# Mixer of a hybrid block: attention pairs two slots behind, bias and maximum in one VectorE instruction, scaling and gate on GpSimd, norms on ScalarE

## The chip, the cores and the metric

The kernel runs on one NeuronCore of one Trainium2 chip. The metric is the device time of one execution in microseconds; lower is better. Six phases run one after the other: pool0, conv, mla, pool1, mixer, ffn. The change touches the mixer alone, and, at its edges, the way the phase in front of the ffn is entered.

## The reference, cut to what matters

The mixer takes 512 tokens of 1024 features, projects them to 27 tiles of 128 columns, and computes three things from them: sliding-window attention with sinks (4 heads of 64), block attention with a linear distance bias (4 heads of 64), and a gated delta rule (4 heads of 128) in chunks of 64 tokens.

```python
scores = jnp.einsum('bnqhgd,bnshd->bnhgqs', qb, kk) * (d ** -0.5)
scores = scores - m * rel                                  # linear bias, masked outside the window
mx = jnp.maximum(scores.max(axis=-1, keepdims=True), sink)
p = jnp.exp(scores - mx)
denom = p.sum(axis=-1, keepdims=True) + jnp.exp(sink - mx)
...
qkv_c = jax.nn.silu(causal_depthwise_conv_2(qkv_c, dn_conv_w))
qc = l2_norm(qc);  kc = l2_norm(kc)                        # x * rsqrt(sum(x*x) + eps), per head
...
def step(state, xs):                                       # one chunk of 64 tokens
    v_new = u_c - w_c @ state
    o = qd_c @ state + a_c @ v_new
    state = state * exp(gl_c) + kd_c.T @ v_new
...
o_c = rms_norm_2(o_c, dn_norm) * jax.nn.silu(z_c)
mixed = jnp.concatenate([o_a, o_b, o_c], axis=-1);  return mixed @ w_out
```

With 512 tokens every block of 256 keys that lies before a query is selected, so the block attention is plain causal attention with the bias.

## The kernel before, in words

Everything lies in SBUF as features x tokens, in tiles of 128 x 512. A projection tile is a product of 8 blocks; each block is three fp32r matmuls (L626 to L628: high part by high, high by low, low by high). The weights stream through a ring of four slots: a DMA on SyncE fills `w_stage`, ScalarE copies it to `w_hi` (L1152, `his(n)`), GpSimd subtracts to `w_lo` (L569, `lo_units`), TensorE uses both and frees the slot. ScalarE works its queue in order, so where `his` stands among its other work decides when the next weights are there; it runs up to four units ahead, and a tile takes two.

The order of the mixer's work is written out by hand in `mixer_steps()`, which lists the steps of TensorE, VectorE and ScalarE; each step raises a semaphore of its engine and the others wait for its number.

- **Front** (`project_in(13)` L668, VectorE L1813 to L1817, ScalarE L1330 to L1339): 8 tiles that pass a causal convolution of width 4 on VectorE (`conv_tile`, L1799: one take, one tensor_scalar, three L1807), a SiLU and a square on ScalarE; one tile for beta and decay; 4 more convolution tiles. The first three tiles are made together, block by block.
- **Delta products** (`delta_products`, L895): the other 14 tiles with the sums of squares (`ssk`, `ssq`), the transpose of the beta and decay rows (`rowt`, L909), and the products of the delta rule in between. ScalarE takes the square roots of the norms (L1359, L1363), VectorE the reciprocals (L1834) and multiplies (L1836, L1838).
- **Inverse** (`inverse`, L941): five levels of 128 x 128 products (L888) for the triangular inverse of all heads.
- **Chunk loop** (L1070): per chunk c the state recurrence `nv` (L978, L981) -> `vn` (ScalarE, L1440) -> `o` and `su` (L989, L993, L999) -> `st` (VectorE, L1971), and two attention pairs k = 2c and 2c + 1 of 16. A pair is two heads of one block of 128 queries, over w = 128 to 512 keys. `attend` (L1004) makes the scores (L1019) and adds the bias as a second matmul of a scaled identity with a distance table (L1021). VectorE reduces the maximum (L1956) and corrects it (L1959 to L1963), ScalarE takes the exponentials with their sums (L1416), VectorE divides (L1948, L1950), TensorE transposes (L1033), ScalarE copies (L1427), TensorE multiplies with the values (`values`, L1050), ScalarE copies to `mixed` (L1435). The scores of pair k, the transpose of k - 1 and the values of k - 2 share a slot.
- **Tail** (L1085 to L1096): two more rounds for the last pairs, the norm of the delta output (`osqrt`, `orc`, `ornt` L1091, `orn`, `ob` L1095), its gain and gate on VectorE (L2001, L2003), the split of `mixed` into parts (`act_h` L1461, `act_l` L1990), and the out projection, tile after tile.

In SWA pairs (k < 8) both heads of a pair lie in the same half of the partitions and their scores in one PSUM bank; in the pairs from 8 on they lie in different halves and banks.

Of the kernel before, what the change touches and what calls it, by code (L numbers as in the profile page):

```python
# [147 lines left out]

HEADS = range(4)
CHUNKS = S // CHUNK  # L150
PAIRS = 16


def mixer_steps():
# [6 lines left out]
    dve = ["ydt", ("kf", 0), ("kf", 1), "beta", "g", ("kf", 2), ("kf", 3), "cols", ("qf", 0), "cd"] + each("kb")  # L161
    dve += [("qf", 1)] + each("dt") + [("qf", 2), ("qf", 3)] + each("kbe") + each("lt", "xt0") + each("at")
    dve += each("e1") + each("qd")
    act = ["tanh", "e1", "ln", "nega"] + each("sk") + each("sq") + each("zs") + ["cexp", "ckd"] + each("egl", "edt")
    act += each("vb") + each("kd") + each("xc") + each("eg")
    for l in range(1, LEVELS):
        pe += each(f"y{l}") + each(f"p{l}")
        dve += (each(f"e{l + 1}") if l < LEVELS - 1 else []) + each(f"xt{l}")
        act += each(f"yc{l}")
    pe += each("wt")  # L170
    act += each("nw")
    dve += ["slopes"]
# [4 lines left out]
    def attend(k):  # L177
        if 1 <= k <= PAIRS:
            dve.append(("nr", k - 1))
        if k < PAIRS:  # L180
            pe.append(("s", k))
            dve.append(("mx", k))
            act.append(("ex", k))

    def turn(k):
        if 1 <= k <= PAIRS:
            pe.append(("t", k - 1))
            act.append(("pc", k - 1))

    def values(k):  # L190
        if 2 <= k:
            pe.append(("pv", k - 2))
            act.append(("mc", k - 2))

    for c in range(CHUNKS):
        act += [("vn", c)]
        attend(2 * c)
        pe += [("nv", c)]
        turn(2 * c)
        pe += [("o", c)] + ([("su", c)] if c < CHUNKS - 1 else [])  # L200
        act += [("oc", c)]
        dve += [("st", c)] if c < CHUNKS - 1 else []
        if c % 2:
            act += [("osq", c // 2)]
        values(2 * c)
        attend(2 * c + 1)
        turn(2 * c + 1)
        if c % 2:
            pe += [("osum", c // 2)]
        values(2 * c + 1)  # L210
    for k in (PAIRS, PAIRS + 1):
        attend(k)
        turn(k)
        values(k)
    pe += ["ornt"] + each("ob")
    act += ["osqrt"]
    dve += ["orc", "orn"] + each("on")
# [34 lines left out]
def program(nc, x_in, stream, params_in, consts_in, consts2_in, pos_in, out, phases):  # L252
    ctx = ExitStack()
    with ctx:
# [26 lines left out]
        probs = sb("probs", [P, 2, 2, S], F32, late)  # L281
        slope_ident = sb("slope_ident", [P, 8, P], F32, late)
# [13 lines left out]
        w_lo = sb("w_lo", [P, RING, S], F32R)  # L296
# [308 lines left out]
        def _(pe):  # L605
# [431 lines left out]
            def values(k):  # L1037

                if k < 2:
                    return  # L1040
# [1242 lines left out]
```

## Time and profile before

| | us |
|---|---|
| runs shown | 2353.81, 2356.09, 2356.20 (median 2356.09) |
| profiled execution, its own time | 2356.29 |
| its span, first to last instruction | 2354.5 |
| TensorE busy | 2269.4 (96%) |
| VectorE / ScalarE / GpSimd busy | 1206.3 / 886.3 / 1031.4 |
| mean granted TensorE clock | 0.981 of full |

The mixer lies from about 1503 to about 1947 us of the span. The granted clock has two levels: 1.00 is 2.4 GHz, 0.50 is 1.2 GHz, and a stretch between is a mean of both.

### The profile page before, as it was taken

To read this page: it belongs to the slowest core of one execution; us is meant where nothing else is said; L and a number is where in the kernel's file an instruction comes from. 1 tells how busy PE (TensorE), PEld (TensorE's weight loads), DVE (VectorE), ACT (ScalarE), POOL (GpSimd) and SP (SyncE) were. 2 spreads that over 40 slices of the span, in tenths; PEclk is the share of its full clock that TensorE was granted. 3 is DMA by queue.
4 is the path that set the end of the run, shared out by engine and by line. 5 is a ranking of instruction groups with operands and counts; after the bars stand their busy time and mean duration, and the time that the engine had idled before them with its cause. 6 is when DMAs were issued, how large, how long until landed. Compare 5 with 4: busy or idle time off the path is not lost.

```text
span 2354.5 us, 32284 instructions
## 1 busy us (share of the span) xinstructions
PE 2269.4 (96%) x10448; PEld 1816.3 (77%) x10448; DVE 1206.3 (51%) x1573; ACT 886.3 (38%) x1546; POOL 1031.4 (44%) x753
## 2 busy tenths in 40 slices
PE   8999999999999999999999999989999887999996
PEld 6788888888888887777887888776896565777785
DVE  7832234444432635555267223496754348888613
ACT  4343343344343434444333443334423323323322
POOL 5654444544544444443456544443200032555553
PEclk9999999999999999999999999999999889999998
DMA  3332323233222222111322322222100021222332
GB/s 133 98 99 98 98 91 99 96 98 98 98 96 96 95 93 72 54 63 36 99 90 89 107 98 93 101 89 72 55 1 1 1 72 45 90 97 89 102 104 98
DMA packets 53643, 194.46 MB, mean 83 GB/s; under 512 B 6080, under 2 KB 6336, under 8 KB 53568
## 3 DMA queue, kind: packets, MB, share of 16 engines
q1 hardware_dynamic: 52560, 191.13, 24.8%
q10 hardware_dynamic: 1008, 2.33, 0.3%
q8 instruction: 47, 0.77, 0.1%
q14 instruction: 28, 0.23, 0.0%
HBM read 191.34 MB, written 2.10 MB: 82 GB/s over the span
## 4 chain that ended last, share of the span: by engine, by line
PE 49%; issue 35%; POOL 15%; DVE 1%; POOLq 1%; ACT 0%; ACTq 0%; DVEq 0%
POOL w_lo L569 15%; PE proj L626 13%; PE proj L627 13%; PE proj L628 13%; PE aux L771 1%; PE proj L796 1%; PE proj L725 1%; PE proj L727 1%; PE proj L726 1%; PE aux L774 1%; PE aux L782 1%; PE proj L753 0%; PE proj L755 0%; PE proj L754 0%; PE proj L743 0%
## 5 line engine op out<-in xcount | busy, mean ns | idle before, releaser
L569 POOL TENSOR_TENSOR w_lo<-w_stage,w_hi 128x512 fp32r<-128x512 f32 x716 | 990.4, 1392 | 1226.1 <-ACT w_hi L1152 1225.5
L1152 ACT ACTIVATE w_hi<-w_stage 128x512 fp32r<-128x512 f32 x716 | 437.1, 627 | 761.9 <-PE proj L628 706.3
L626 PE MATMUL proj<-xh,w_hi 128*128 128x512 f32 x1696 | 672.6, 397 | 19.0 <-POOL w_lo L569 16.9
L627 PE MATMUL proj<-xl,w_hi 128*128 128x512 f32 x1696 | 662.0, 390 | 0.0
L628 PE MATMUL proj<-xh,w_lo 128*128 128x512 f32 x1696 | 661.8, 390 | 0.0
L626 PEld LDWEIGHTS proj<-xh,w_hi 128*128 128x128 f32 x1696 | 319.3, 188 | 106.0 <-POOL w_lo L569 34.1
L628 PEld LDWEIGHTS proj<-xh,w_lo 128*128 128x128 f32 x1696 | 319.1, 188 | 67.6
L627 PEld LDWEIGHTS proj<-xl,w_hi 128*128 128x128 f32 x1696 | 319.5, 188 | 66.8 <-issue 2.4
L626 PE MATMUL proj<-act_h,w_hi 128*128 128x512 f32 (+1 forms) x864 | 337.7, 391 | 0.6 <-POOL w_lo L569 0.6
L627 PE MATMUL proj<-act_l,w_hi 128*128 128x512 f32 (+1 forms) x864 | 336.9, 390 | 0.0
L628 PE MATMUL proj<-act_h,w_lo 128*128 128x512 f32 (+1 forms) x864 | 336.9, 390 | 0.0
L626 PEld LDWEIGHTS proj<-act_h,w_hi 128*128 128x128 f32 x864 | 162.7, 188 | 37.5 <-issue 2.5
L628 PEld LDWEIGHTS proj<-act_h,w_lo 128*128 128x128 f32 x864 | 162.7, 188 | 33.9
L627 PEld LDWEIGHTS proj<-act_l,w_hi 128*128 128x128 f32 x864 | 162.8, 188 | 33.5
L1220 ACT ACTIVATE act_h<-prod 128x512 f32 (+1 forms) x102 | 64.5, 632 | 258.9 <-DVE prod L2037 130.9
L1566 DVE TENSOR_TENSOR ssum<-ssum,sq 128x512 f32<-128x512 f32 x64 | 63.9, 998 | 150.5 <-ACT sq L1158 150.1
L1607 DVE TENSOR_TENSOR x_res<-proj,x_res 128x512 f32 x32 | 22.1, 692 | 218.3 <-PE proj L628 217.1
L1637 DVE TENSOR_TENSOR act_l<-prod,act_h 128x512 f32 (+1 forms) x102 | 82.0, 804 | 85.8 <-ACT act_h L1220 85.8
L2043 DVE TENSOR_TENSOR z<-proj,rstd 128x512 f32<-128x512 f32 x32 | 22.1, 692 | 112.7 <-PE proj L628 111.9
L583 POOL TENSOR_SCALAR pr<-pr,small 128x128 f32<-128x128 f32 (+3 forms) x32 | 40.8, 1275 | 76.0 <-DVE small L1737 76.0
L1267 ACT ACTIVATE pr<-aux,small 128x128 f32<-128x128 f32 (+3 forms) x64 | 33.2, 524 | 53.2 <-DVE small L1730 53.1
L2086 DVE SCALAR_TENSOR_TENSOR yg<-gpad,params_sb,yg 128x512 f32<-128x512 f32 x44 | 49.9, 1133 | 6.5 <-DVE yg L2084 3.4
(313 smaller groups left out, 2413.4 us busy)
## 6 DMA issues: line engine op xcount, KB each, us to landing
w_stage<-stream SPq DMA_DIRECT2D x358, 512.0 KB, 3.3
out<-x_res SPq DMA_DIRECT2D x4, 512.0 KB, 2.6
x_res<-x SPq DMA_DIRECT2D x2, 512.0 KB, 8.3
consts_sb<-consts ACTq DMA_DIRECT2D x1, 832.0 KB, 4.4
x_res<-x ACTq DMA_DIRECT2D x1, 512.0 KB, 7.4
x_res<-x SPq DMA_DIRECT2D x1, 256.0 KB, 3.3
x_res<-x ACTq DMA_DIRECT2D x1, 256.0 KB, 5.1
pos_i<-pos ACTq DMA_DIRECT2D x1, 256.0 KB, 2.7
```

The costliest lines, as they stand in the source:

```text
L569: pool.tensor_tensor(w_lo[:, at, :], w_stage[:, at, :], w_hi[:, at, :].bitcast(F32), ALU.subtract).then_inc(stage_free, 1)
L583: pool.tensor_scalar(pr[:, qb % 2, 0, 0:w], pr[:, qb % 2, 0, 0:w], stat(INVERSE, qb)[:, 0:1], None, ALU.mult).then_inc(probs_done, 1)
L626: pe.matmul(o, w_hi[:, slot, cols], hi, start=(b == 0), stop=False)
L627: pe.matmul(o, w_hi[:, slot, cols], lo, start=False, stop=False)
L628: mm = pe.matmul(o, w_lo[:, slot, cols], hi, start=False, stop=(b == blocks - 1))
L725: pe.matmul(o, w_hi[:, slot, cols], lat_h[:, k, :], start=(b == 0), stop=False)
L1152: act.activation(w_hi[:, u % RING, :], w_stage[:, u % RING, :], ACT.Copy).then_inc(hi_done, 1)
L1220: act.activation(act_h[:, slot, :], prod[:, :], ACT.Copy).then_inc(ah_done, 1)
L1267: e = act.activation(pr[:, qb % 2, h, 0:w], score_banks(qb, w)[:, h, :], ACT.Exp, bias=stat(BIAS, qb)[:, h:h + 1], scale=SCALE, accum_out= ...
L1566: dve.tensor_tensor(total[:, :], total[:, :], sq[:, (sqs.n - 1) % 2, :], ALU.add).then_inc(ssum_done, 1)
L1637: dve.tensor_tensor(act_l[:, slot, :], prod[:, :], act_h[:, slot, :].bitcast(F32), ALU.subtract).then_inc(al_done, 1)
L2086: return dve.scalar_tensor_tensor(yg[:, t, :], gpad[:, t, 2:2 + S], par("ffn_conv_w", f + 4 * FT), yg[:, t, :], ALU.mult, ALU.add)
```

## The change

It is in ten places, all in the mixer:

1. The 17 front tiles have a new order (`FRONT`): v0 v1 v2 z0 v3 k0 z1 k1 k2 z2 k3 ba q0 z3 q1 q2 q3. The four gate tiles z stood in `delta_products` before. ScalarE now issues `his` for tile i + 1 before it takes tile i's SiLU.
2. `ssk` stands after 14 tiles, `ssq` five tiles later; one tile stands between the further products where two or three stood.
3. The norms: ScalarE takes Ln of the sums (`sk`, `sq`), then Exp with scale -0.5 (`rk`, `rq`); VectorE's eight reciprocals L1834 go. The SiLUs of the gates no longer stand between the others, so ScalarE loads fewer tables.
4. The distance tables times the slopes are written by ScalarE (8 `fill` steps) during the inverse. The bias matmuls L1021 and `slope_ident` go.
5. The maximum: two `tensor_tensor_reduce` per pair add the bias in place in PSUM and reduce, in place of L1956 to L1963. The sink's exponential is two ScalarE instructions.
6. Pairs are (t, t + 2) for SWA: the heads of every pair lie in different halves of the partitions, their scores in different banks.
7. The division of the probabilities is on GpSimd (two instructions per pair); `probs` has three buffers. The transpose lags by two pairs, the values by three.
8. GpSimd also multiplies the delta outputs by the gate (4 instructions), so L2003 goes.
9. `SLOTS`: slots 0 to 5 hold two pairs, 6 and 7 one, and pairs 14 and 15 come after. The splits of `mixed` 0, 1 and 2 are made as soon as they are complete; the reciprocal of the final norm moves ahead of the loop.
10. The out projection makes its first three tiles together, block by block in the order 0 1 2 4 5 6 7 3.

The diff, cut to its core:

```diff
+FRONT = ("v0", "v1", "v2", "z0", "v3", "k0", "z1", "k1", "k2", "z2", "k3", "ba", "q0", "z3", "q1", "q2", "q3")
+OUT_ORDER = (0, 1, 2, 4, 5, 6, 7, 3)
+SLOTS = ((0, 1), (2, 3), (4, 5), (6, 7), (8, 9), (10, 11), (12,), (13,))
+AFTER_STEPS = (14, 15)
...
@@ gpsimd
+            n = n_units(phases[:phases.index("mixer") + 1]) - RING - 2 * DT + RING
+            lo_units(first, n - first)
+            for k in range(PAIRS):
+                w = pair_of(k)[3]
+                pool.wait_ge(mix_dve, DVE_STEP["rs", k])
+                for t in range(2):
+                    ins = pool.tensor_scalar(probs[:, k % 3, t, 0:w], probs[:, k % 3, t, 0:w], soft[:, k % 2, 1, t:t + 1],
+                                             None, ALU.mult)
+                ins.then_inc(pair_scaled, 1)
+                if k % 4 == 3 and k < 15 or k == 13:
+                    blk = min(k // 4, 3)
+                    pool.wait_ge(mix_act, ACT_STEP["osq", blk])
+                    pool.tensor_tensor(mixed[:, 4:8, blk * P:blk * P + P], mixed[:, 4:8, blk * P:blk * P + P],
+                                       zc[:, :, blk * P:blk * P + P], ALU.mult).then_inc(gated, 1)
+            lo_units(n, units - n)
...
@@ tensor: one slot
+                for c, slots in enumerate(SLOTS):
+                    a, b = slots[0], slots[-1]
+                    attend(a)
+                    new_values(c)
+                    if b > a:
+                        attend(b)
+                    if a == 2:
+                        pe.wait_ge(mix_act, ACT_STEP["avc", 3])
+                    turn(a - 2)
+                    output_and_update(c, a - 4)
+                    values(a - 3, c)
+                    if b > a:
+                        turn(b - 2)
                     if c % 2:
+                        output_sums(c // 2, a - 3)
+                    if b > a:
+                        values(b - 3, c)
+                for k in AFTER_STEPS:
                     attend(k)
+                    turn(k - 2)
+                    values(k - 3, CHUNKS - 1)
+                turn(PAIRS - 2)
+                pe.wait_ge(mix_act, ACT_STEP["osqrt"])
+                values(PAIRS - 3, CHUNKS - 1)
                 pe.wait_ge(mix_dve, DVE_STEP["orc"])
...
@@ scalar: norms and exponentials
-                    made(act.activation(squares8[:, h, :], head_bank(h, 0), ACT.Sqrt, bias=con("eps")), ("sk", h))
+                    made(act.activation(squares8[:, h, :], head_bank(h, 0), ACT.Ln, bias=con("eps")), ("sk", h))
...
+                for h in HEADS:
+                    made(act.activation(squares8[:, h, :], squares8[:, h, :], ACT.Exp, scale=-0.5), ("rk", h))
...
+                    act.wait_ge(mix_dve, DVE_STEP["mx", k])
+                    if k >= 2:
+                        act.wait_ge(pair_scaled, k - 1)
...
@@ vector
+                    for t, head in enumerate(pair_heads(tl)):
+                        scores = pair_scores(k)[:, t, :]
+                        ins = dve.tensor_tensor_reduce(scores, scores, bias_of(k, head), -1.0,
+                                                       less_sinks[:, 2 * tl + t:2 * tl + t + 1] if tl < 2 else 3e38,
+                                                       ALU.add, ALU.min, soft[:, k % 2, 0, t:t + 1])
+                    made(ins, ("mx", k))
...
                 for c, slots in enumerate(SLOTS):
+                    if a:
+                        scale_of(a - 1)
+                    maxima(a)
+                    if b > a:
+                        scale_of(a)
+                        maxima(b)
+                    scaled_x(c)
                     if c < CHUNKS - 1:
                         dve.wait_ge(mix_pe, PE_STEP["su", c])
...
@@ out projection
-                    project_out(DT, 2, al.n)
+                    together(of_mixed, lambda k: pe.wait_ge(al_done, al.n + k + 1), DT)
+                    for t in range(DT - TOGETHER):
+                        products(tile.n % BANKS, DT, of_mixed)
```

## Rows read from the trace of the kernel before

**Rows 1.** The page: busy time of each engine, its share of the span.
```profile
PE 2269.4 (96%) x10448; PEld 1816.3 (77%) x10448; DVE 1206.3 (51%) x1573; ACT 886.3 (38%) x1546; POOL 1031.4 (44%) x753
```
**Rows 2.** Windows: stretch, us; busy of PE, PEld, DVE, ACT, POOL; PEclk; DMA; GB/s.
```profile
1523.80:1565.20 41.40, 34.21 (x144) 26.43 (x144) 38.77 (x44) 17.25 (x30) 15.35 (x12) 1.00 0.23 75
...
1610.50:1623.10 12.60, 8.33 (x30) 6.75 (x31) 8.81 (x8) 1.26 (x2) 2.73 (x2) 0.73 0.12 42
...
1751.30:1776.60 25.30, 21.06 (x71) 13.79 (x72) 10.02 (x26) 5.94 (x18) 0.00 (x0) 0.60 0.00 0
1776.60:1857.40 80.80, 79.63 (x533) 58.31 (x532) 35.49 (x110) 33.96 (x101) 0.00 (x0) 1.00 0.00 1
1857.40:1888.20 30.80, 24.03 (x83) 12.46 (x83) 10.46 (x18) 9.93 (x19) 0.00 (x0) 0.63 0.00 1
1888.20:1936.70 48.50, 45.90 (x193) 37.48 (x192) 20.19 (x21) 15.27 (x26) 20.70 (x16) 0.95 0.24 76
```
**Rows 3.** Timeline of TensorE: start, us, operation; in brackets the idle time before.
```profile
1551.62 0.50 PE L626 MATMUL proj<-xh,w_hi 128*128 128x512 f32 x1 [1.51 <-POOL w_lo L569]
...
1614.77 0.71 PE L909 MATMUL aux<-consts_sb,rows 68*128 68x68 f32 x4 [4.28 <-DVE rows L1863]
```
**Rows 4.** Groups by form, 1600 to 1950: busy us, mean ns, idle before.
```profile
L1834 DVE RECIPROCAL squares<-squares 128x512 f32<-128x512 f32 x8 | 26.8, 3353 | 6.7 <-ACT squares L1359 6.5
...
L1359 ACT ACTIVATE squares<-aux,consts_sb 128x512 f32<-128x512 f32 x4 | 2.8, 689 | 0.1
...
L1367 ACT ACT_TABLE_LOAD x1 | 1.3, 1283 | 0.0
```
**Rows 5.** Timeline of TensorE in the loop: scores and bias of a pair.
```profile
1805.28 0.70 PE L1019 MATMUL aux<-a_kv,a_q 64*128 64x256 f32 x2
1805.91 0.70 PE L1021 MATMUL aux<-consts_sb,slope_ident 128*128 128x256 f32 x2
...
1831.03 1.12 PE L1021 MATMUL aux<-consts_sb,slope_ident 128*128 128x512 f32 x2
1832.08 1.12 PE L1019 MATMUL aux<-b_k,b_q 64*128 64x512 f32 x2
```
**Rows 6.** Timeline of TensorE in the mla phase: two heads' 64-row matmuls in turn.
```profile
1085.68 0.70 PE L774 MATMUL aux<-k_rot,qr 64*128 64x256 f32 x4
...
1099.28 1.13 PE L774 MATMUL aux<-k_rot,qr 64*128 64x512 f32 x4
1100.34 0.49 PE L796 MATMUL proj<-pt,v_heads 128*128 128x128 f32 x2
```
**Rows 7.** Timeline of TensorE: first matmul of chunks 2 and 7.
```profile
1787.79 0.43 PE L978 MATMUL proj<-vbeta,xt 128*64 128x128 f32 x2
...
1852.30 0.43 PE L978 MATMUL proj<-vbeta,xt 128*64 128x128 f32 x2
```
**Rows 8.** Timeline of VectorE and ScalarE: the recurrence, chunk 4.
```profile
1829.78 1.12 DVE L1971 SCALAR_TENSOR_TENSOR state<-state,egl,proj 128x128 f32<-128x128 f32 x4 [4.13 <-PE proj L999]
...
1826.37 0.59 ACT L1440 ACTIVATE vnew<-proj 64x512 f32<-64x512 f32 x1 [3.32 <-PE proj L981]
```
**Rows 9.** Groups by form on VectorE, 1750 to 1890, and on GpSimd.
```profile
L1956 DVE TENSOR_REDUCE soft<-aux 128x2 f32<-128x1024 f32 x2 | 2.4, 1224 | 9.6 <-PE aux L1021 9.6
...
L583 POOL TENSOR_SCALAR pr<-pr,small 128x512 f32<-128x512 f32 x8 | 14.8, 1853 | 33.3 <-DVE small L1737 33.3
...
L583 POOL TENSOR_SCALAR pr<-pr,small 128x256 f32<-128x256 f32 x8 | 8.7, 1087 | 3.8 <-DVE small L1737 3.8
```
**Rows 10.** Timeline of TensorE in the loop: products with the values.
```profile
1835.63 0.66 PE L1050 MATMUL proj<-probs_t,v_tok 128*64 128x128 f32 x8
...
1847.43 1.58 PE L1050 MATMUL proj<-probs_t,v_tok 128*64 128x128 f32 x16
```
**Rows 11.** Timeline of TensorE: a gap in the loop; the out projection's start.
```profile
1857.41 0.44 PE L1050 MATMUL proj<-probs_t,v_tok 128*64 128x128 f32 x4 [0.69 <-ACT mixed L1444]
...
1888.18 0.80 PE L626 MATMUL proj<-act_h,w_hi 128*128 128x512 f32 x1
```

More of the change, by code:

```diff
@@ L175, in mixer_steps @@
         act += [("avc", blk)]
[L177 to L199, printed above, removed]
-        pe += [("o", c)] + ([("su", c)] if c < CHUNKS - 1 else [])
[L201 to L207, printed above, removed]
+    dve += ["rf"]
@@ L218, in mixer_steps @@
+    act += ["osqrt"]
+    dve += [("rs", PAIRS - 1), "orc", "orn"] + each("on")
+    turned(PAIRS - 2)
+    valued(PAIRS - 3)
+    pe += ["ornt"]
+    turned(PAIRS - 1)
+    valued(PAIRS - 2)
+    pe += each("ob")
+    valued(PAIRS - 1)
     return pe, dve, act
@@ L967, in inverse, with attend, new_values @@
                                    lambda blk: xt[:, h, blk, :]), ("wt", h))
-            def chunk(c):
+            def attend(k):
+                _, qb, first, w = pair_of(k)
+                tl = k // 4
+                if k >= 2:
+                    pe.wait_ge(mix_act, ACT_STEP["ex", k - 2])
+                for t in range(2):
+                    part = slice(64 * t, 64 * t + 64)
+                    q, keys = (a_q[part, tl, :], a_kv[part, 0, :]) if tl < 2 else (b_q[part, tl - 2, :], b_k[part, tl - 2, :])
+                    mm = pe.matmul(pair_scores(k)[:, t, :], q[:, qb * P:qb * P + P], keys[:, first:first + w],
+                                   start=True, stop=True)
+                made(mm, ("s", k))
+            def new_values(c):
                 blk, r = c // 2, CHUNK * (c % 2)
@@ L1197, in out_tiles, with grouped_out_tiles_of_y @@
                 deviation(ahead, twice)
+            def grouped_out_tiles_of_y():
+                for t in range(DT):
+                    his(2 * TOGETHER if t == 0 else 2 if t >= TOGETHER else 0)
+                    act.wait_ge(slot_free, unit.now())
+                    square(proj[:, tile.n % BANKS, :])
+                    tile.up()
+                deviation(False)
             def out_tiles_of_y(per_tile):
@@ L1609, in out_tiles, with grouped_out_tiles_of_y @@
                 deviation(twice)
+            def grouped_out_tiles_of_y(post):
+                dve.wait_ge(slot_free, unit.now() + RING + 2 * TOGETHER)
+                for t in range(DT):
+                    b = bank(2)
+                    add_square()
+                    take(dve.tensor_scalar(y[:, t, :], b, par(post, t), None, ALU.mult))
+                deviation()
             def out_tiles_of_y(per_tile, post):
@@ L1811, in conv_tile @@
                     dve.wait_ge(conv_done, n + 1)
-                for i in range(8):
-                    conv_tile(i, (i + 4) % 8)
-                take(dve.tensor_tensor(raw[:, :], bank(2), rstd[:, :], ALU.mult))
-                for i in range(4):
-                    conv_tile(8 + i, 8 + i)
                 def made(ins, name):
@@ L1965, in hybrid_mixer, with scale_of @@
-                for c in range(CHUNKS):
-                    attend(2 * c)
+                dve.wait_ge(std_done, stds.n)
+                made(dve.reciprocal(r_final[:, :], r_final[:, :]), "rf")
+                def scale_of(k):
+                    sums = soft[:, k % 2, 1, :]
+                    dve.wait_ge(mix_act, ACT_STEP["ex", k])
+                    if k < 8:
+                        link(dve.tensor_tensor(sums, sums, soft[:, k % 2, 2, :], ALU.add))
+                    made(dve.reciprocal(sums, sums), ("rs", k))
```

522 lines of the change are left out of this document (279 added, 243 removed).

## The prediction, made blind

> **What bounds the kernel now.** I read the page first: TensorE is busy 96% of the span and no other engine over 51% [rows 1], so time can be won in two ways only, fewer or shorter matmuls, or less TensorE idle time and less time at the low clock. Windows over the mixer say where both lie [rows 2]. The input side (1523.80 to 1565.20) has TensorE busy 34.21 of 41.40 us. From 1751.30 to 1776.60 the granted clock is 0.60, and from 1857.40 to 1888.20 it is 0.63 (0.50 is 1.2 GHz, 1.00 is 2.4 GHz). Between them TensorE is busy 79.63 of 80.80 us at full clock: the chunk loop is bound by its matmuls, although they are small. The timeline gives the idle time before single matmuls: four gaps of 1.5 us behind the weight ring in the front (the first is shown) and 4.28 us in front of the transposed rows, which wait for VectorE [rows 3].
>
> The profiled execution took 2356.29 us, of which 1.8 lie outside the span; the median of the runs is 2356.09, so a sum made against the one holds for the other within 0.2.
>
> **The change, part by part.**
>
> *Front and delta products.* The 27 tiles and all products stay. The four 1.5 us gaps come from ScalarE, which issues each weight copy behind a SiLU that waits for a convolution on VectorE. With gate tiles in between VectorE gets one cheap tile in three, and `his` now stands ahead of the previous tile's SiLU; a tile takes TensorE 5.45 us (24 matmuls of 0.228), a convolution about 5 us of VectorE, so the copy is due before it is needed: -6.0, and -0.3 of small gaps. The 4.28 us gap came from a chain ScalarE (four table changes of 1.28) to VectorE (two of the eight 3.35 us reciprocals stood ahead of the decay rows) [rows 4]. After, the rows are ready some 17 us after the last front tile and TensorE asks for them at 22. In its place I see one new wait: `ssq` needs its bank from `sk`, and ScalarE reaches `sk` only after q3's SiLU and square (7.0 after TensorE's last front tile), tanh 0.6, two weight copies 1.2, two table loads with three small activations 4.1 and one Ln of 0.69 [rows 4]: 13.6, while TensorE has done its two further tiles at 10.9. So 4.28 becomes 2.7. The slow stretch behind that gap (clock 0.73 over 12.6 us, 6.8 us at half, 3.4 lost [rows 2]) I keep at 2.0, as a shorter gap may or may not cause it. Sum: -6.3 - 1.6 - 1.4 = -9.3. The added Exps (8 of 0.63) lie beside tiles on ScalarE, which is busy 33.51 of 74.3 us there. Bounds: -12 if the clock holds, -3 if `ssq` and VectorE's later steps are later by another 3 and the clock falls twice.
>
> *Fills.* Eight copies on ScalarE (at most 0.6 each, by its other 128x512 instructions) in the inverse, two a level, while TensorE makes products for 53.9 us and ScalarE is busy 14.15 of them; the next level's copy is due 7 us later. Nothing; at most 0.6 a level, 2.4, if that cover is gone. The reciprocal of the final norm, 3.35, now runs under the last products of the inverse.
>
> *Scores.* One score or bias matmul (two instructions) takes 0.63 us at w = 256 and 1.05 at 512 from start to start [rows 5]; 128 and 384 lie at 0.415 and 0.84. A pair has four: 1.66, 2.5, 3.36, 4.2. After, it has two, on different halves of the partitions, one behind the other. The mla phase has just this form: four instructions of two heads take 0.70 at 256, and 1.06 at 512 from start to start [rows 6], so the two heads run side by side, and a pair costs 0.42, 0.63, 0.84, 1.06. Saved: SWA 2 x (1.24 + 3 x 1.87) = 13.7, the others 2 x (1.24 + 1.87 + 2.52 + 3.15) = 17.6, together 31.3. The other bound is no overlap: 20.9.
>
> *Values.* Now block by block, heads alternating. At 8 instructions they take 0.66, at 16 1.58 [rows 10]. Eight others of this width would take 0.9, so heads on different columns overlap already, fully at 8 and in part at 16; if 12 and 16 become as good as 8, -0.2 and -0.4 for two pairs each: -1.3. The Trainium skill ("TensorE: Matmul & The Clock Gate", Part 3) says matmuls keep strict order of start and end. By that the old order could overlap only where the head changes, and the new one would halve all 68 products, about -6. The row at 8 speaks against it, and I take -1.3 and leave it inside the rounding.
>
> *A slot after.* TensorE, SWA at full clock: two scores 1.26, `nv` 1.74, transposes 1.0, `o` and `su` 2.9, values 1.2, half an `osum` 0.45: 8.5. Before, chunks 2 to 6 take (1852.30 - 1787.79)/5 = 12.9 [rows 7]. What becomes late next is the recurrence. From the start of `nv`: ScalarE ends `vn` at 2.7, `o` and `su` end at 4.8, `st` 1.12 ends at 6.1 [rows 8]. But VectorE works in order: in front of `st` stand `rs(a)`, which waits for ScalarE's `ex(a)` at 4.0, `mx(b)` and the scaled x of 0.75, so `st` ends at about 7.4 and ScalarE copies values at 7.1 to 7.7, where TensorE would want them 0.2 earlier. So slots run at 8.3 to 9.4, TensorE still the bound but by less than 1 us. The unseen instruction is the `tensor_tensor_reduce`. VectorE takes 1.04 ns per element column and 0.16 fixed for one fp32 result from PSUM; 1024 columns reduced take 1224 ns [rows 9]. Below: 0.43 at 256, 0.69 at 512; above: twice that, as if two passes. I take the lower, nearest to the row, plus 0.1. At the upper bound every slot gets 0.9 to 1.4 longer on VectorE, about half of it seen: +5.
>
> *GpSimd.* A scaling takes 1087 ns at 256 and 1853 at 512 [rows 9], a pair 2.2 to 3.7, a gate 1.4; per slot at most 8.8 of 9, mostly 5, and the transpose comes two pairs later. It is off the path in the loop. At the end it is on it: pairs 14 and 15. The Trainium skill ("GPSIMD Engine Reference", 4.1 Engine selection) calls one-input instructions roughly line-rate; by that a pair would cost under 1 us and the tail be shorter by 3. The rows of the mla phase say three to four times the price of VectorE, and they decide.
>
> *Sum of loop and tail.* Counted from the first scores, all at full clock: chunk 1 starts at 6.4 (idle 1.5 in it, a bare recurrence), chunk 7 at 56.0, the last slot ends at 62.5. Then: s14, t12, pv11, s15, t13, pv12 to 67.2; t14 waits for GpSimd until 69.6; `osqrt` behind a table load 71.9; pv13, ornt 73.0; t15 waits for GpSimd's 3.7 until 73.7; pv14, ob, pv15 and its copy: 81.5. Before it is 133.3 (1754.9 to 1888.18 [rows 11]). This 81.5 is only to be had at 2.4 GHz.
>
> *The clock.* Before, the loop begins with 20 us at 1.2 GHz after gaps of 0.3 to 0.8; a gap of 0.69 at 1857.41 [rows 11] is followed by about 7 us at half, and the tail falls twice more. A slot after has waits of 0.2 to 0.6 each and lighter matmuls. At half clock, TensorE's 8.5 becomes about 15 (rows of the first window: a score pair of 2.5 takes 4.6). I add: start as before, 8.5; two to four falls of 7 us in the loop, each costing 3, 9; tail 6. Together 81.5 + 23.5 = 105, against 133.3: -28.3. Bounds: +0 (81.5, -52) and all at half (136, +3).
>
> *Out projection.* 192 matmuls of 0.228 as before. It starts with parts 0, 1, 2, ready early, 6.2 us of work, and the delta parts come every 1.5 to 1.8 us against 2.05 of work. Before, 4 us of it were slow; after, perhaps 6: +1. The phase's end and the way into ffn stay.
>
> Sum: -9.3 - 28.3 + 1 = -36.6, from 2356.3: **2319.7**.
>
> **Rivals.**
> (a) *The clock holds*: TensorE leaves fewer gaps than I think, as it does over 80 us now [rows 2]. Front -12, loop and tail 81.5 to 93: 2293 to 2305. For it: TensorE stays the bound of a slot. Against: the margin is under 1 us.
> (b) *The loop runs at 1.2 GHz for most of its length*: removed matmuls come back as half speed, slots of 14 to 15 us. 105 becomes about 134: 2348. For it: 0.69 us was enough at 1857. Against: at half clock TensorE has no gaps, and before the clock came back from such stretches.
> (c) *VectorE or ScalarE is the bound of the slot*: the new instruction at its upper price, or more handovers than counted, slots of 11 instead of 9: + 15: 2335.
> (d) *Slower*: case (b), and the low clock goes on into the out projection, 43.8 us at full clock, which gains a microsecond for each it spends at half clock. With (b) at 2348 it decides from 8 us on; at 17 us: 2365. Against: the dense stretch from 1888.20 has clock 0.95 now [rows 2].
> That the bias matmuls would be hidden anyway is ruled out by 79.63 of 80.80 us.
>
> **How the numbers follow.** Forecast (2308 to 2332) 0.55, (a) 0.2, (b) 0.1, (c) 0.1, (d) 0.05. From 2297 to 2342 the range holds the forecast, most of (a) and all of (c), 0.8. A measurement of this kernel can tell 0.2%, 4.7 us, from no change: within that lies a part of (b) and (d), 0.03; slower 0.03; faster 0.94.
>
> **What would show it.** In the trace after: no gaps of 1.5 us before 1566, and `y1` of the inverse 8 to 12 us earlier; an idle time before `ssq` released by ScalarE's Ln; two heads' scores of w = 256 in 0.7 us; chunk starts 8.3 to 9.4 us apart where the clock is 1.00; loop and tail 93 to 117 us long; idle time before t(14) and t(15) released by GpSimd. I am wrong if the scores of two heads don't overlap, if chunk starts lie over 11 us apart at full clock, if the reduce instruction takes over 0.8 us at 256, or if the clock over the loop is under 0.65.

## The result, and the profile after

The changed kernel takes 2299.53 us (median of 4 runs, 2298.37 to 2300.52), the kernel before 2355.20 beside it: ratio 0.9764, 95% interval 0.9749 to 0.9779, 55.7 us less. Forecast were 36.6 less, 2319.7, with a range from 2297 to 2342: inside the range, at its fast end, where rival (a) had put it (2293 to 2305). The profiled execution took 2300.2, its span is 2298.4, 56.1 less than before.

| stretch | before | after | difference | forecast |
|---|---|---|---|---|
| fourth front tile to first scores | 230.23 | 217.51 | -12.7 | -9.3 |
| first scores to out projection (loop and tail) | 133.27 | 91.53 | -41.7 | -28.3 |
| out projection, to the statistics | 48.53 | 48.46 | -0.1 | +1 |
| everything else of the span | 1942.5 | 1940.9 | -1.6 | 0 |

The page's busy times, after, to be held against [rows 1]:

```profile
PE 2224.7 (97%) x10384; PEld 1799.7 (78%) x10384; DVE 1168.0 (51%) x1538; ACT 894.3 (39%) x1567; POOL 1066.4 (46%) x789
```

The windows of the mixer after, columns as in [rows 2]: front tiles without a gap; the stretch at the sums of squares; seven slots of the loop; loop and tail as a whole; out projection.

```profile
1524.16:1609.54 85.38, 85.38 (x368) 69.05 (x368) 69.59 (x69) 35.43 (x58) 41.48 (x29) 1.00 0.26 88
1609.54:1623.00 13.46, 11.48 (x39) 7.51 (x40) 4.02 (x6) 12.63 (x19) 3.15 (x3) 0.87 0.22 78
...
1748.20:1804.80 56.60, 54.53 (x418) 45.43 (x419) 25.33 (x94) 31.09 (x94) 24.62 (x25) 0.91 0.00 1
...
1741.67:1833.20 91.53, 82.08 (x610) 64.85 (x609) 37.52 (x131) 48.26 (x140) 35.63 (x36) 0.89 0.00 1
1833.20:1881.60 48.40, 45.79 (x192) 37.46 (x192) 19.25 (x22) 16.91 (x29) 20.71 (x16) 0.96 0.23 76
```

A window with its PEclk gives a number that the rest of this text goes by: length times granted clock is what the stretch would take with the clock up throughout, and the remainder is what the clock took. Two things blur it: the granted clock is given to a hundredth, half a microsecond or so here, and where TensorE waits while the clock is low the remainder is too large, by 0.4 to 1.6 us in most of these kernels, 2.2 in number 4 and 2.7 in the kernel before. The whole loop and tail before, as one window, and after, row above: 133.27 x 0.84 = 111.9 and 21.3 for the clock; 91.53 x 0.89 = 81.5 and 10.1.

```profile
1754.91:1888.18 133.27, 122.77 (x672) 83.28 (x673) 55.95 (x154) 47.26 (x132) 0.00 (x0) 0.84 0.00 1
```

TensorE's timeline after: two heads' scores in one row, the first matmuls of chunks 1 to 3, and the waits that are left.

```profile
1611.52 5.37 PE L932 MATMUL aux<-squares,ones 128*128 128x512 f32 x8 [1.98 <-ACT squares L1437]
...
1743.11 0.70 PE L1006 MATMUL aux<-a_kv,a_q 64*128 64x256 f32 x4
1748.17 0.43 PE L1018 MATMUL proj<-vbeta,xt 128*64 128x128 f32 x2 [1.76 <-DVE state L2098]
1757.67 0.43 PE L1018 MATMUL proj<-vbeta,xt 128*64 128x128 f32 x2
1766.29 0.43 PE L1018 MATMUL proj<-vbeta,xt 128*64 128x128 f32 x2
1774.13 1.02 PE L1084 MATMUL proj<-ones,osq 128*128 128x1 f32 x8 [0.89 <-ACT mixed L1526]
1787.93 1.13 PE L1006 MATMUL aux<-b_k,b_q 64*128 64x512 f32 x4
1794.38 1.02 PE L1084 MATMUL proj<-ones,osq 128*128 128x1 f32 x8 [0.95 <-ACT mixed L1526]
1813.78 1.09 PE L1071 MATMUL proj<-probs_t,v_tok 128*64 128x128 f32 x16
1819.96 1.16 PE L1057 MATMUL proj<-consts_sb,probs 128*128 128x128 f32 x6 [2.38 <-ACT probs_t L1519]
```

Against [rows 5]: 0.70 us held two instructions at w = 256 and holds four now; 1.13 at 512. The four gaps of [rows 3] are gone, and the 4.28 in front of the rows has become 1.98 in front of `ssq`, released by ScalarE's logarithms.

VectorE's and GpSimd's new instructions, by form (busy, mean ns of one, idle before):

```profile
L2066 DVE CUSTOM_DVE_ANT_0 aux<-aux,bias_b 128x512 f32<-128x512 f32 x4 | 2.7, 715 | 0.1
L2066 DVE CUSTOM_DVE_ANT_0 aux<-aux,bias_b 128x256 f32<-128x256 f32 x4 | 1.6, 449 | 0.1
L2066 DVE DVE_READ_ACCUMULATOR2_ANT soft<- 128x1 f32 x32 | 4.6, 142 | 0.0
```
```profile
L632 POOL TENSOR_SCALAR probs<-probs,soft 128x256 f32<-128x256 f32 x16 | 14.6, 922 | 19.7 <-DVE soft L2059 19.7
L632 POOL TENSOR_SCALAR probs<-probs,soft 128x512 f32<-128x512 f32 x4 | 6.2, 1562 | 2.2 <-DVE soft L2059 2.2
```

### The profile page after: what moved, and what is told of

The parts are those of the page before. It is cut to its first block, busy times and chain, and to the rows that moved or that the text cites. A ratio compares the mean times of both kernels' runs of the same rounds, so it can differ in the third digit from the quotient of the medians.

```text
span 2298.4 us, 32107 instructions
## 1 busy us (share of the span) xinstructions
PE 2224.7 (97%) x10384; PEld 1799.7 (78%) x10384; DVE 1168.0 (51%) x1538; ACT 894.3 (39%) x1567; POOL 1066.4 (46%) x789
## 3 DMA queue, kind: packets, MB, share of 16 engines
q1 hardware_dynamic: 52560, 191.13, 24.7%
## 4 chain that ended last, share of the span: by engine, by line
PE 71%; issue 17%; POOL 9%; DVE 2%; ACT 1%; POOLq 0%; ACTq 0%; DVEq 0%
PE proj L665 18%; PE proj L666 18%; PE proj L667 18%; POOL w_lo L594 9%; PE aux L799 2%; PE proj L824 1%; PE proj L916 1%; PE aux L916 1%; PE proj L753 1%; PE proj L755 1%; PE proj L754 1%; PE aux L802 1%; PE aux L810 1%; PE proj L1018 0%; PE aux L1006 0%
## 5 line engine op out<-in xcount | busy, mean ns | idle before, releaser
L665 PE MATMUL proj<-xh,w_hi 128*128 128x512 f32 x1696 | 671.2, 396 | 11.8 <-POOL w_lo L594 9.7
L665 PE MATMUL proj<-act_h,w_hi 128*128 128x512 f32 (+1 forms) x840 | 327.6, 390 | 0.6 <-POOL w_lo L594 0.6
L667 PE MATMUL proj<-act_h,w_lo 128*128 128x512 f32 (+1 forms) x840 | 327.3, 390 | 0.0
L666 PE MATMUL proj<-act_l,w_hi 128*128 128x512 f32 (+1 forms) x840 | 327.3, 390 | 0.0
L665 PEld LDWEIGHTS proj<-act_h,w_hi 128*128 128x128 f32 x840 | 157.8, 188 | 34.7 <-issue 1.0
L667 PEld LDWEIGHTS proj<-act_h,w_lo 128*128 128x128 f32 x840 | 157.8, 188 | 32.7
L666 PEld LDWEIGHTS proj<-act_l,w_hi 128*128 128x128 f32 x840 | 157.8, 188 | 32.3
L2156 DVE TENSOR_TENSOR z<-proj,rstd 128x512 f32<-128x512 f32 x32 | 22.1, 692 | 112.7 <-PE proj L667 111.9
L632 POOL TENSOR_SCALAR probs<-probs,soft 128x256 f32<-128x256 f32 (+3 forms) x32 | 30.4, 962 | 105.3 <-DVE soft L2059 105.3
```

The lines of the kernel that those rows point to most:

```text
L665: pe.matmul(o, w_hi[:, slot, cols], hi, start=(b == 0), stop=False)
L666: pe.matmul(o, w_hi[:, slot, cols], lo, start=False, stop=False)
L667: mm = pe.matmul(o, w_lo[:, slot, cols], hi, start=False, stop=(b == blocks - 1))
```

## The experiments

All are edits of the changed kernel; a time without a comparison stands against its 2299.53. Each profile is of one execution. The intervals are 3.5 us wide to either side or more, so a difference of 3 to 4 us between two variants rests on their runs not overlapping (changed 2298.37 to 2300.52, number 3 2301.74 to 2303.68, number 6 2294.60 to 2297.48). The table gives each one's ratio to the kernel before with its interval, and of its profile the length of loop and tail, the granted clock in it, and their product.

| kernel | us | ratio (95%) | loop and tail | clock | product |
|---|---|---|---|---|---|
| before | 2355.20 | 1 | 133.3 | 0.84 | 111.9 |
| changed | 2299.53 | 0.9764 (0.9749 to 0.9779) | 91.5 | 0.89 | 81.5 |
| bias_back | 2318.52 | 0.9845 (0.983 to 0.986) | 106.2 | 0.90 | 95.6 |
| bias_serial | 2337.26 | 0.9921 (0.9903 to 0.9938) | 129.2 | 0.83 | 107.2 |
| old_loop | 2344.31 | 0.9952 (0.9934 to 0.997) | 135.7 | 0.82 | 111.2 |
| scale_dve | 2302.28 | 0.9776 (0.9761 to 0.9791) | 95.2 | 0.86 | 81.8 |
| lag_one | 2306.90 | 0.9797 (0.9782 to 0.9812) | 98.5 | 0.85 | 83.7 |
| mc_first | 2295.85 | 0.9748 (0.9735 to 0.9761) | 86.6 | 0.92 | 79.6 |
| tail_order | 2296.12 | 0.975 (0.9736 to 0.9763) | 90.0 | 0.88 | 79.2 |
| best | 2292.84 | 0.9732 (0.9718 to 0.9745) | 90.1 | 0.88 | 79.2 |

**1. bias_back.**

```diff
-                                   start=True, stop=True)
+                                   start=True, stop=False)
+                for t, head in enumerate(pair_heads(tl)):
+                    mm = pe.matmul(pair_scores(k)[:, t, :], con("ident", P), bias_of(k, head), start=False, stop=True)
...
+                    link(dve.tensor_reduce(nmax, pair_scores(k), AX.X, ALU.max))
```

> The bias goes back to TensorE: after the two score matmuls of a pair (they stay side by side) two matmuls of the identity with the head's bias table are added into the same bank; VectorE reduces the maximum with the plain reduce and corrects it, as before the change. All else is the changed kernel. The bias matmuls of a pair cost TensorE 2 x 0.415, 0.63, 0.84, 1.05 us for w = 128 to 512, over 16 pairs 21.0 us. Theory A (TensorE still bounds the slots): the loop and tail grow from 91.5 us by 15 to 21, slots at full clock from 8.6 to about 11; the kernel takes 2315 to 2320 against 2299.5. Theory B (the slots are already bound by the handovers between the engines): the matmuls fill idle time of TensorE, loop and tail grow by 3 to 9, 2303 to 2308.

Loop and tail grew by 14.7 and the median by 19.0; the profiled execution, the fastest of the four, grew by 15.8. Theory A, just under its lower end: of 21.0 us forecast for the matmuls 14.1 are seen at full clock. TensorE's busy time grew by 17.0 and its waits shrank by 2.3 (9.5 to 7.2, window below against the one above); most of the last 4 is a price that was put too high. The bias matmuls of two heads, issued one behind the other, take about 1.06 us at w = 256 from start to start and not twice 0.63, and about 0.2 less than the price at the other widths too: some 18 us over the loop and not 21.0.

```profile
1740.98:1847.20 106.22, 99.03 (x673) 74.49 (x673) 40.16 (x107) 48.31 (x140) 35.96 (x36) 0.90 0.00 1
...
1760.34 1.13 PE L1009 MATMUL aux<-cy,consts_sb 128*128 128x256 f32 x4
```

**2. bias_serial.** Each head's bias matmul directly behind its score matmul.

> As the run with the bias on TensorE (2318.52; loop and tail 106.2), with each head's bias matmul right behind its score matmul, so that no two score matmuls of different partition halves stand side by side. All matmuls stay. Theory A (two 64-row matmuls on different halves run side by side, as the first score rows of the changed kernel say): each pair costs TensorE 0.415 to 1.05 us more, 10.3 over the loop, of which 7 to 10 is seen: loop and tail 113 to 117, 2326 to 2329. Theory B (TensorE overlaps them in this order as well, or the slots hide it): under 3.

Loop and tail 129.2, 23 more than in 1, far over both theories. The product splits it: 11.6 more at full clock and another 11.4 for the clock (in this one execution; the median grew by 18.7). The 11.6 are not the score matmuls alone. By the rows each head's score now takes 0.63 from start to start at w = 256, so two heads no longer overlap: 10.5 over the loop. But the edit parts the bias matmuls too, and each head's now takes 0.63 as well (0.70 with its end, row below, against 1.13 for both in number 1): 3.1. Of these 13.6 the length shows 11.6. The windows show the whole stretch; 3.4 us up to just before a fall of the clock and 3.4 us in which it falls, both without any wait of TensorE; and 27.3 us at half clock in which it was busy 24.7:

```profile
1741.09:1870.28 129.19, 122.76 (x674) 84.26 (x673) 39.24 (x107) 48.31 (x140) 35.95 (x36) 0.83 0.00 1
1757.00:1760.40 3.40, 3.40 (x30) 2.97 (x29) 1.83 (x7) 3.03 (x10) 0.17 (x2) 1.00 0.03 7
1760.40:1763.80 3.40, 3.40 (x16) 2.93 (x16) 1.55 (x3) 0.24 (x1) 2.92 (x3) 0.59 0.00 0
1835.50:1862.80 27.30, 24.72 (x78) 12.40 (x80) 4.48 (x9) 7.59 (x18) 6.54 (x5) 0.51 0.00 1
...
1752.47 0.70 PE L1006 MATMUL aux<-a_kv,a_q 64*128 64x256 f32 x2
1753.10 0.70 PE L1008 MATMUL aux<-cy,consts_sb 128*128 128x256 f32 x2
```

**3. scale_dve.** The division on VectorE, GpSimd keeps the gate.

```diff
-                        made(dve.reciprocal(sums, sums), ("rs", k))
+                        link(dve.reciprocal(sums, sums))
+                        for t in range(2):
+                            ins = dve.tensor_scalar(probs[:, k % 3, t, 0:w], probs[:, k % 3, t, 0:w], sums[:, t:t + 1],
```

> The division of the probabilities goes back from GpSimd to VectorE (two tensor_scalars of 0.28 to 0.48 us behind the reciprocal, from the rows of the kernel before); the lag of the transposes stays two pairs. Theory A (the slot is TensorE's, the tail is GpSimd's): a slot's state update comes about 1.4 us later on VectorE, of which some 0.5 is seen per slot, +3 over the loop; in the tail the waits of 0.63 and 2.37 us for the last pairs go, -3; together 2297 to 2302. Theory B (taking the division off VectorE is what makes the short slots): slots longer by the whole 0.7 to 1.0 us per pair, +8 to +11 over the loop: 2306 to 2310.

2302.28, 2.8 us more, just above theory A's 2302; B is out. At full clock the loop is as long as with GpSimd (81.8 against 81.5); in the profiled executions the difference lies in the clock. So the move to GpSimd, taken alone, brought at most these 2.8 us and no shorter work. A's reason fails for the tail: the wait before pair 14's transpose did not go with GpSimd, since ScalarE releases it.

```profile
1825.53 1.54 PE L1061 MATMUL proj<-consts_sb,probs 128*128 128x128 f32 x6 [2.60 <-ACT probs_t L1523]
```

**4. lag_one.** Number 3 with `turn(a - 1)` and `values(a - 2)` for `turn(a - 2)` and `values(a - 3)`, on all engines.

> As the run with the division on VectorE (2302.28, loop and tail 95.1), and the transposes lag by one pair instead of two, the values by two instead of three, as before the change. Theory A (the lag is what keeps the waits short, and short waits keep the clock): TensorE waits 1 us or more in each slot for the division of the pair just made, and the granted clock is at half for 15 us or more in the first slots as before; loop and tail 103 to 115. Theory B (with the bias matmuls gone the lag matters little): 95 to 98, and the tail is shorter by a pair's turn, so it may be equal.

98.5, just above theory B's 95 to 98, and under A's 103: 1.9 more at full clock than number 3, and 4.6 in the kernel's median. The lag matters little. TensorE does wait longer, 12.9 us in all against 9.9 in number 3, in the slots for example:

```profile
1760.88 1.02 PE L1086 MATMUL proj<-ones,osq 128*128 128x1 f32 x8 [1.11 <-ACT mixed L1526]
1772.15 1.12 PE L1073 MATMUL proj<-probs_t,v_tok 128*64 128x128 f32 x8 [0.80 <-ACT mixed L1526]
```

**5. old_loop.** Numbers 2 and 4 together.

> The run above with the division on VectorE and the lag of one pair: the whole attention of the loop as before the change, in the new slots and with the new norms. Measured alone, bias 14.7, division 3.6 and lag 3.4 were added to 91.5, and the serial order is expected at 10: 123. Theory A (they add up): 120 to 126 for loop and tail, half clock for 20 us or less in it: 2332 to 2337. Theory B (together they bring the long stretch at half clock of the kernel before, 20.5 us, back): 128 to 135, 2340 to 2346.

135.7, the upper end of theory B's length and far over A's. But A's 123 had the serial order at 10 us, and number 2 has since shown 23. With the prices measured one by one the parts do add up, as A said. The raw lengths give 91.5 + 14.7 + 23.0 + 3.7 + 3.3 = 136.2, the medians of the kernels 2344.6 for 2344.31 (so close by luck, its eight runs go from 2339.05 to 2353.44), the products 81.5 + 14.1 + 11.6 + 0.3 + 1.9 = 109.4 for 111.2 (the kernel before has 111.9), and the clock's shares 26.7 for 24.4. B's reason, the 20.5 us at half clock in the first slots, did not come back: the longest such stretch ahead of the last slot is 10.2.

```profile
1741.77:1877.44 135.67, 125.72 (x674) 86.76 (x673) 47.53 (x139) 48.53 (x140) 5.05 (x4) 0.82 0.00 1
```

**6. mc_first.**

```diff
+                    valued(a - 3)
                     if b > a:
                         exponentials(b)
-                    valued(a - 3)
```

> In a slot ScalarE copies the values of pair a-3 before it takes the exponentials of pair b, not behind them. TensorE waits 0.89 and 0.95 us for that copy in slots 3 and 5 (before the sums of squares), and each time the granted clock falls to half for 3.4 us right behind. Theory A (the falls come from these waits): the waits shrink to under 0.4, the two falls go with them, 1.3 + 2 x 1.7 = 4 to 5 us less: 2294 to 2296. Theory B (the falls come anyway, or move to the next gap): only the idle time is won, 2298.

3.7 us less, and 5.0 in the loop and tail: theory A, for the slots. The waits of 0.89 and 0.95 are gone; from 1750.20 to 1804.80 TensorE waits 0.5 us in all and the clock stays up, where the changed kernel has 2.1 us of waiting and clock 0.91 (its third window above).

```profile
1750.20:1804.80 54.60, 54.09 (x456) 45.45 (x456) 27.73 (x101) 34.15 (x101) 26.99 (x29) 1.00 0.01 2
```

One wait of 1.76 at the start of chunk 1 is the same in both:

```profile
1750.18 0.43 PE L1019 MATMUL proj<-vbeta,xt 128*64 128x128 f32 x2 [1.76 <-DVE state L2099]
```

In the changed kernel the clock fell for 3.4 us right behind it, here it did not. So a wait of that length may or may not bring a fall; and by number 2's windows a fall can come with no wait at all. This missing fall, 1.7 us, is in the 5.0 and is not the edit's. Against it stands a fall of 6.8 us behind a wait of 0.53, where the changed kernel has none:

```profile
1805.77:1812.58 6.81, 6.35 (x32) 4.64 (x34) 1.31 (x5) 1.80 (x6) 1.01 (x1) 0.50 0.00 0
```

That it is one of the two, moved, is not excluded by this trace alone; numbers 8, 10 and 11 have a fall at about the same point of the work without the edit, so it does not need it. In numbers 7 and 12, which have the edit too, no fall stands behind the sums in slots 3 and 5 either.

**7. tail_order.** Number 6, and ScalarE and TensorE work the last pairs in this order:

```diff
+    pe += [("s", 14), ("t", 12), ("pv", 11), ("s", 15), ("t", 13), ("pv", 12), ("t", 14), ("pv", 13), "ornt",
+           ("pv", 14), ("t", 15)] + each("ob") + [("pv", 15)]
+    act += [("pc", 12), ("ex", 14), ("mc", 11), ("pc", 13), ("mc", 12), ("ex", 15), ("mc", 13), "osqrt",
+            ("pc", 14), ("mc", 14), ("pc", 15), ("mc", 15)]
```

> The run with ScalarE's copy of values first (2295.85, loop and tail 86.6), and the tail in another order: ScalarE copies the transposes of pairs 12 and 13 and the values of 12 before the exponentials of pair 15; transpose and values of pair 13 come before the square root of the norm; the values of pair 14 before the transpose of 15. What it tells apart: whether the two waits of 2.77 and 1.02 us in the tail are ScalarE's order (theory A: they shrink to under 1 together, and half of a fall goes: 3 to 5 us less, loop and tail 82 to 84, 2291 to 2293) or GpSimd's division of pairs 14 and 15 (theory B, as forecast: the wait stays with GpSimd as its releaser, 0 to 1.5 less).

Theory A was right on the first wait, wrong on the gain: 2296.12, no change (loop and tail are 3.4 longer in the profiled execution, all of it clock). The wait for the transpose of pair 14 fell from 2.77 to 0.43, now with GpSimd as its releaser; 2.60 us turned up one step later, at the reciprocal that VectorE takes behind the square root of the norm, so that 3.8 us of waiting became 3.0.

```profile
1813.72 0.84 PE L1050 MATMUL proj<-consts_sb,probs 128*128 128x128 f32 x6 [0.43 <-POOL probs L625]
1817.75 0.60 PE L1119 MATMUL proj<-consts_sb,rc 128*4 128x128 f32 x4 [2.60 <-DVE rc L2103]
```

**8. his_behind.** `front_tile(i)` directly behind tile i's copies, in place of `front_tile(i - 1)`.

> Only the order on ScalarE in the front is undone: the weight copies of tile i+1 stand behind tile i's SiLU again; the gate tiles stay between the convolution tiles. Theory A (the gate tiles do most of it: with one cheap tile in three VectorE is ahead, so ScalarE's wait for a convolution is short): one or two gaps of up to 1 us return, +1 to +2, the first inverse product at 1686 to 1687 instead of 1684.9. Theory B (the place of the copy does it): a gap of 1.5 us returns after each convolution tile that follows another, four or more, +6: 1691.

The front grows by 1.7 us (219.20 for 217.51), with two smaller gaps (1.16, 0.52) and 2.82 us before `ssq` where 1.98 stood: theory A there. The changed kernel's front holds a fall of the clock that cost 1.7, and this one has none, so at full clock it is 3.4 longer. The median, 2304.60, is 5.1 above; the rest lies in no stretch that the edit touches (in the profiled execution loop and tail are 1.4 longer, and the mixer begins 1.2 later).

**9. gates_last.** The four z tiles at the end of `FRONT`.

> Only the order of the front tiles is undone: the four gate tiles come after the last convolution tile; the weight copies stay ahead of the SiLU. Theory A of the run above: VectorE, at about 5 us a convolution against 5.45 a tile, keeps up without them, and the copies no longer wait, so no gap of 1.5 returns; the decay rows are ready earlier; 0, within 1.5 us either way. Theory B (without gates between them the convolutions fall behind and TensorE waits for a free bank or for weights): +3 to +6.

The front grows by 0.8 (218.29), at full clock by 2.5, and the kernel takes 2302.18, 2.7 more. The length is theory A's, but for another reason than either theory's: two gaps of 1.5 come back, behind the weights, and the wait for `ssq` shrinks from 1.98 to 0.37, since ScalarE ends the front with a cheap gate tile.

```profile
1557.35 0.50 PE L665 MATMUL proj<-xh,w_hi 128*128 128x512 f32 x1 [1.47 <-POOL w_lo L594]
1561.88 0.50 PE L665 MATMUL proj<-xh,w_hi 128*128 128x512 f32 x1 [1.51 <-POOL w_lo L594]
...
1615.02 3.67 PE L932 MATMUL aux<-squares,ones 128*128 128x512 f32 x8 [0.37 <-ACT squares L1437]
```

**10. front_old.** Numbers 8 and 9 together.

> Both edits of the front are undone together: weight copies behind the SiLU, and the gate tiles after the convolution tiles. Alone the first cost 1.7 us and the second 0.8 between the fourth front tile and the first inverse product (160.7 in the changed kernel). Theory A (each covers for the other): together they bring back at least four gaps of 1.5 us, 5 to 7 us, not the sum of 2.5: 2305 to 2307 against 2299.5. Theory B (additive): +2.5, 2302.

Theory A by the front's length: 222.60, 5.1 more, twice the sum of 8 and 9. Four gaps are back, as in [rows 3], together 6.8, less 1.6 at `ssq`. But the changed kernel's fall of the clock hides in all three differences: at full clock they are 3.4, 2.5 and 6.8 against its 215.8, almost a plain sum, and the kernel's median, 2304.38, is not above that of number 8. Only the gaps behind the weights are clearly more than those of 8 and 9 added (1.7 and 3.0). That the two edits cover for each other in time is not shown.

```profile
1551.55 0.50 PE L665 MATMUL proj<-xh,w_hi 128*128 128x512 f32 x1 [2.30 <-POOL w_lo L594]
1556.07 0.50 PE L665 MATMUL proj<-xh,w_hi 128*128 128x512 f32 x1 [1.50 <-POOL w_lo L594]
```

**11. recip_back.**

```diff
-                    made(act.activation(squares8[:, h, :], head_bank(h, 0), ACT.Ln, bias=con("eps")), ("sk", h))
+                    made(act.activation(squares8[:, h, :], head_bank(h, 0), ACT.Sqrt, bias=con("eps")), ("sk", h))
...
+                    link(dve.reciprocal(lengths, lengths))
```

> The norms as before the change: ScalarE takes square roots, VectorE eight reciprocals of 3.35 us, each in front of its multiply; no Exps for them on ScalarE. Front order and all else as in the changed kernel. Theory A (the reciprocals would be on the path now): the keys' four reciprocals, 13.4 us, stand between the columns and the key-times-beta products that TensorE's second row spread waits for, and TensorE has two tiles of 5.45 and one spread there: +5 to +10, partly at half clock, 2305 to 2310. Theory B (VectorE has slack there, 4.28 us of waiting came from their place in front of the decay rows alone): 0 to +2, 2299 to 2302.

2314.00, 14.5 more, over theory A; the front takes 229.26, 11.8 more, of which 5.1 is the clock. The keys' reciprocals hold VectorE up, and TensorE waits for the first `kb` product, which stands behind the norms of all four:

```profile
1646.09 7.19 PE L907 MATMUL aux<-rows,consts_sb 64*128 64x512 f32 x8 [4.89 <-DVE mixed L1991]
```

Over the stretch around it, the clock is down as well, by 0.15 x 47 = 7 us:

```profile
1615.00:1662.00 47.00, 41.40 (x136) 26.49 (x136) 36.75 (x42) 13.95 (x26) 10.13 (x8) 0.85 0.13 45
```

This is not the order of the kernel before, where some of the reciprocals ran earlier beside more tiles; it says that the new order of the tiles needs the new norms.

**12. best.** Number 7, and

```diff
+FRONT = ("v0", "v1", "v2", "z0", "v3", "k0", "z1", "k1", "k2", "k3", "ba", "q0", "q1", "q2", "q3", "z2", "z3")
```

> ScalarE's copy of values first, the other order of the tail, and the front with two gate tiles early and two behind the last convolution (z0 after v2, z1 after k0, z2 and z3 last). The run with all gates last had 0.37 us of waiting for the sums of squares instead of 1.98, but two gaps of 1.5 between its early convolutions; the changed kernel has the early gates and no such gap. Theory A (both can be had): neither, so 1.6 us less and, where the granted clock stays up, 1.7 more: front 214 to 216 us from the fourth tile to the first scores, 217.5 in the changed kernel; with the loop 2291 to 2294. Theory B (the gate tiles are needed between the later convolutions too): one or two gaps of 1.5 come at k2 or k3 and q1, 2296 to 2298.

Theory A in the front: 214.21 us, no gap of 1.5, and the wait for `ssq` is 0.37. Of the 3.3 us less, 1.6 is this wait and 1.7 a fall of the clock that is missing here; numbers 1, 2, 3 and 7 lack it too, with the front of the changed kernel untouched.

```profile
1609.88 3.67 PE L925 MATMUL aux<-squares,ones 128*128 128x512 f32 x8 [0.37 <-ACT squares L1430]
```

At 2292.84 (2291.25 to 2293.83) it is the fastest, 6.7 us under the changed kernel and 3.0 under number 6.

## Why the prediction came out as it did

**The work of the loop: right, the exact total in part by luck.** Forecast at full clock 81.5, measured 81.5. Its parts: the bias matmuls 14.1 (number 1) and the serial order 11.6 more (number 2), together 25.7 of the forecast 31.3. The price of the matmuls was right (some 18 and 13.6 us of TensorE by the rows of numbers 1 and 2, against 31.3), but not all of it is seen in the length. Counted at full clock from the first scores, chunk 7 starts at 57.8 where 56.0 was forecast, and the rest takes about 24 for 25.5: two errors that cancel. Chunk 1 starts 6.5 us after the first scores (6.4 forecast), chunk 3 comes 8.62 after chunk 2 (8.3 to 9.4). The values of 16 instructions take 1.09 us, 1.58 before [rows 10]: the 1.3 of the forecast, and a little. Those of 8 take 0.66 as before, so nothing is seen of the 6 us that halving all products would have brought.

**The clock: the step that was mis-sized.** The forecast added 23.5 us; it was 10.1. Of its three terms the start was put at 8.5, "as before": there was one fall of 3.4 us, costing 1.7. In the loop "two to four falls of 7 us": there were two of 3.4. The tail, 6, cost 5. This is 13.4 of the 19.1 us that the forecast fell short. The reason given for it, more waits and lighter matmuls, did not hold: TensorE waits about as long before as after (133.27 - 122.77 = 10.5, 91.53 - 82.08 = 9.5), and with the lighter matmuls the falls are as many, five in loop and tail for four, but last 3.4 to 6.8 us each, where they lasted 6.8 to 20.5. Nor do waits order the experiments: number 2 waits 6.4 us and loses 22, number 6 waits 7.2 and loses 7. The two falls inside the loop went with the two waits before the sums (numbers 6, 7 and 12), so these waits brought them here; but the same waits, of 0.95 to 1.11 us, stand without a fall behind them in numbers 1, 4 and 10. Once a fall inside the loop follows no wait (number 2, in the window from 1760.40, behind transposes, sums of one column and values). In the loop ahead of its last slot only two kernels have stretches of 10 us or more at half clock, the one before (20.5) and number 5 (10.2), the two that have the old attention whole; in the last slot and the tail such stretches come in seven of the twelve variants. What keeps the clock down that long, with TensorE busy, stays open: number 2 says only that another order of the same matmuls can bring it (its median lies 18.7 above number 1's, with 11.6 of work).

**The front: right in place, short by 3.4.** At full clock it went from 226.8 to 215.8. The four gaps went (-6.0), 4.28 became 1.98 where 2.7 was forecast, released by ScalarE's logarithms as said, and the slow stretch cost 0.13 x 13.46 = 1.7 for 3.4 [rows 2]. Of the other 2.7 us, 0.3 had been forecast; the `g1` products take 3.7 for 4.7, a wait of 0.64 ahead of the first scores is gone, and 0.8 was not followed up. The credit for the edits was given too simply: without the early copies 3.4 us of the 11.0 at full clock go, without the gate tiles between 2.5, without both 6.8, and without the norms 6.6 (numbers 8 to 11).

**The out projection.** Forecast was 1 longer, with 6 us at half clock; it is 0.1 shorter, and its clock is 0.96 where it was 0.95.

**VectorE's new instruction: right.** It takes 0.449 us at 256 (0.491 in the twelve that start from the sinks) and 0.715 at 512, and the read of its result 0.142 more, partly beside it; forecast were 0.53 and 0.79 in all, the upper bound was 0.86 and 1.38. Rival (c) fell with it.

**GpSimd: right on the price, wrong on the tail.** A division takes 0.92 at 256 and 1.56 at 512, less than [rows 9], but 2.6 and 3.2 times the 0.35 and 0.48 of VectorE in the kernel before; hidden in the loop as forecast, and its move away from VectorE worth at most 2.8 us (number 3). By the Trainium skill ("GPSIMD Engine Reference", 4.1 Engine selection) one-input instructions are roughly line-rate; the trace disagrees by that factor. The wait before pair 14's transpose is there, 2.38 us, but its releaser is ScalarE: it copied pair 13 behind the exponentials of 15. Number 7 took that away, and only then GpSimd was last, with 0.43.

**Rivals.** (a) was nearest, with its reason half right: the clock did not hold, it fell six times for 27 us in all from the front to the start of the out projection, but short. (b) and (d) did not come. What set the forecast apart from (a) is the loss that it carried over from the kernel before. That (a) gives the time is partly luck, since its reason did not hold and the length of the falls stays unexplained.

## What to carry to other kernels

Compare stretches by length times granted clock before explaining a difference, and look at more than one execution: the changed front stands untouched in eight of these kernels and takes 217.5 us in four and 215.8 in four, with or without one short fall behind the same wait of 1.98 us. Before saying that prices do not add up, put measured ones into the sum (number 5). Where a short instruction of a slow engine stands in front of the copy that TensorE waits for, the swap of two lines (number 6) can bring as much as moving a whole operation to another engine, or more (3.7 us against the 2.8 of number 3). Undo edits alone and together before saying what each is worth, and take the clock out of both sides of the sum (numbers 8 to 10).

## What was not expected of the hardware

Two heads' fp32 matmuls with 64 rows each, on different halves of the partitions, run side by side when issued next to each other (0.70 us for both at w = 256), and not when a 128-row matmul stands between them (0.70 each). Two heads' 128-row matmuls of the same width take 1.13 in a row and 0.70 each apart, from start to start 1.06 against twice 0.63, so parting them costs 0.2 us; why is not shown. A wait of 1.76 us was followed by a fall of the granted clock in one execution and by none in another; falls behind waits of 0.9 to 1.1 us lasted from 3.4 to 10.2 us (numbers 1 and 5). And falls come with no wait close ahead: one in number 2, and the last one of the changed kernel's tail, at 1830.65, 3.4 us after the clock had come back:

```profile
1827.24:1830.64 3.40, 3.40 (x8) 1.28 (x8) 1.49 (x2) 0.25 (x1) 0.00 (x0) 1.00 0.00 0
1830.64:1833.20 2.56, 2.12 (x18) 1.58 (x17) 0.00 (x0) 0.30 (x2) 0.00 (x0) 0.50 0.02 6
```
